# Moving the last transposes of a step and the preparation of the next tokens in an expert loop

## The chip, the cores and the metric

The kernel runs on one core of a Trainium2 chip. The metric is the device time of one execution in microseconds (us). Five engines run at once: TensorE (PE, matmuls and transposes), the vector engine (DVE), ScalarE (ACT), GpSimd (POOL) and SyncE (SP), which issues weight transfers. Each works through its own list in order and waits on semaphores that others raise.

## The reference

One layer of a diffusion backbone over 1024 latent tokens of width 1024, with a context of 256: modulation, RMSNorm, a combined projection, windowed and neighbourhood attention, an output projection, and then the part that matters here, a mixture of experts. Each token goes to 4 of 32 experts, and each expert computes

```
hu  = x @ w1[e] + b1[e]                       # 1024 -> 2048
glu = minimum(hu[:, 0::2], 7)
lin = clip(hu[:, 1::2], -7, 7)
act = glu * sigmoid(1.702 * glu) * (lin + 1)
y   = act @ w2[e] + b2[e]                     # 1024 -> 1024
```

The four results of a token are summed with softmax weights, normalised and added to the token. Everything is fp32.

## The kernel before

The kernel runs `front`, `attention`, `middle` (output projection, router, table of steps), `experts` and `combine`. The change is in `experts`.

**Steps.** Tokens of an expert stand in blocks of 128. A step handles one expert with R blocks: R = 1 (a one-block step) or R = 2 (a two-block step). A first loop runs 16 pairs, a one-block step and then a two-block step; a second loop runs 3 one-block steps. `body(st, next_r)` is the code of a step on one engine; `nxt` is the step behind it with `next_r` blocks.

**Units.** The weights of an expert are six units of 1024 x 512, four up (w1, n = 0 to 3) and two down (w2, n = 4, 5). Each is one transfer of 2 MB into a ring of three. fp32 is computed as high and low parts: ScalarE writes `w_hi` (L1256, `split`), the vector engine writes seven eighths of `w_lo` (L1311) and GpSimd the last eighth (L1208). A product of one unit and one block is 8 x 3 matmuls (L1402 to L1404), with a bias matmul ahead (L1418 up, L1436 down).

**Between up and down.** The result of up product j goes to the vector engine, which computes glu (L1356), lin (L1357, L1359) and, with ScalarE's sigmoid (L1286), act_o (L1361). `columns(st, j)` turns it for the down products: TensorE transposes act_o (L1389), ScalarE writes a_hi (L1265), the vector engine a_lo (L1321). It runs one product late: after product j come the columns of j - 1. The last j has no up product behind it. TensorE does it inside the first down unit, for the last block, ahead of k = 6; until then the down product needs only a_hi and a_lo of the earlier j.

**Between steps.** `rows(nxt, r)` prepares block r of the next step: TensorE transposes the gathered rows (L1382) into two PSUM banks, ScalarE writes x_hi (L1260), the vector engine x_lo (L1315). Row 0 follows the last up product, row 1 (if there is one) the first down product of block 0; TensorE's row r waits until x_lo of row r - 1 has been written. ScalarE and the vector engine do row 0 and the last `columns` ahead of their split at n = 4.

**The way back.** ScalarE copies each down product from its bank to y (L1295). There are two banks, so TensorE's down product i waits for the copy of product i - 2. GpSimd scatters y to memory and gathers the rows of the next step.

Of the kernel before, what the change touches and what calls it, by code (L numbers as in the profile page):

```python
# [28 lines left out]
KD = D // P  # L29
# [1053 lines left out]
def experts(K):  # L1083
# [3 lines left out]
    UP, DOWN = 2 * FF // UNIT, D // UNIT  # L1087
# [7 lines left out]
    with ctx:  # L1095
# [23 lines left out]
        at_done, ahi_done, a_ready = sem("at_done"), sem("ahi_done"), sem("a_ready")  # L1119
# [128 lines left out]
        @block.scalar  # L1248
        def _(act):
            act.sem_inc(y_copied, 2)  # L1250

            def split(st, n):
                wait_loaded(act, st, n)
                for c in range(CH):
                    k = slice(KC * c, KC * (c + 1))
                    act.activation(w_hi[:, n % HI, k, :], ring[:, n % RING, k, :], ACT.Copy).then_inc(hi_done, 1)  # L1256

            def rows(st, r):
                act.wait_ge(xt_done, st.blocks + r + 1)
                act.activation(x_hi[:, r, :, :].rearrange("p k n -> p (k n)"), ps[:, 6:8, :].rearrange("p b n -> p (b n)"), ACT.Copy).then_inc(xhi_done, 1)  # L1260

            def columns(st, j):
                act.wait_ge(at_done, UP * st.blocks + j + 1)
                n, r = divmod(j, st.R)
                act.activation(a_hi[:, r, 2 * n:2 * n + 2, :].rearrange("p k n -> p (k n)"), ps[:, 2 + j % 2, 0:2 * P], ACT.Copy).then_inc(ahi_done, 1)  # L1265

            first = Step(1, 0, 0)
            rows(first, 0)
            split(first, 0)
            split(first, 1)  # L1270

            def body(st, next_r):
                nxt = st.then(next_r)
                for n in range(NU):
                    if n == UP:
                        rows(nxt, 0)
                        columns(st, UP * st.R - 1)
                    act.wait_ge(prod_done, units_done(st, n))
                    if n + 2 < NU:
                        split(st, n + 2)  # L1280
                    else:
                        split(nxt, n + 2 - NU)
                    if n < UP:
                        for j in range(n * st.R, n * st.R + st.R):
                            act.wait_ge(glu_done, UP * st.blocks + j + 1)
                            act.activation(sig[:, j % 2, :], glu[:, j % 2, :], ACT.Sigmoid, scale=ALPHA).then_inc(sig_done, 1)  # L1286
                            if j:
                                columns(st, j - 1)
                        continue
                    if n == UP:  # L1290
                        act.wait_ge(y_free, st.passes + 1)
                    h = n - UP
                    for r in range(st.R):
                        wait_product(act, st, n, r)
                        act.activation(y[:, r, h * UNIT:(h + 1) * UNIT], ps[:, 4 + (h * st.R + r) % 2, :], ACT.Copy).then_inc(y_copied, 1)  # L1295
                        if n == UP and r + 1 < next_r:
                            rows(nxt, r + 1)

            program(act, body)

        @block.vector
        def _(dve):
            dve.sem_inc(lo_done, RING * CH)
            dve.sem_inc(up_free, 2)
            dve.sem_inc(a_ready, 2)

            def split(unit, n):
                for c in range(CH):
                    k = slice(KC * c, min(KC * (c + 1), KP))
                    dve.wait_ge(hi_done, CH * unit + c + 1)  # L1310
                    dve.tensor_tensor(w_lo[:, n % LO, k, :], ring[:, n % RING, k, :], w_hi[:, n % HI, k, :].bitcast(F32), ALU.subtract).then_inc(lo_done, 1)  # L1311

            def rows(st, r):
                dve.wait_ge(xhi_done, st.blocks + r + 1)
                dve.tensor_tensor(x_lo[:, r, :, :].rearrange("p k n -> p (k n)"), ps[:, 6:8, :].rearrange("p b n -> p (b n)"),  # L1315
                                  x_hi[:, r, :, :].bitcast(F32).rearrange("p k n -> p (k n)"), ALU.subtract).then_inc(x_ready, 1)

            def columns(st, j):
                dve.wait_ge(ahi_done, UP * st.blocks + j + 1)
                n, r = divmod(j, st.R)  # L1320
                dve.tensor_tensor(a_lo[:, r, 2 * n:2 * n + 2, :].rearrange("p k n -> p (k n)"), ps[:, 2 + j % 2, 0:2 * P],  # L1321
                                  a_hi[:, r, 2 * n:2 * n + 2, :].bitcast(F32).rearrange("p k n -> p (k n)"), ALU.subtract).then_inc(a_ready, 1)

            def select(sel, e, ready):

                col = onehot[:, bass.ds(e, 1)]
                dve.tensor_copy(sel[:, :], col.to_broadcast([96, P])).then_inc(ready, 1)

            first = Step(1, 0, 0)
            rows(first, 0)  # L1330
            dve.wait_ge(bias_loaded, 32)
            select(sel_up, expert_of(dve, first), sel_up_ready)
            split(0, 0)

            def body(st, next_r):
                nxt = st.then(next_r)
                unit = NU * st.passes
                link = linker(dve, dve_own, UP * st.blocks)
                e, e_next = expert_of(dve, st), expert_of(dve, nxt)
                for n in range(NU):  # L1340
                    if n == UP:
                        rows(nxt, 0)
                        columns(st, UP * st.R - 1)
                    dve.wait_ge(prod_done, units_done(st, n))
                    split(unit + n + 1, (n + 1) % NU)
                    if n == 0:
                        select(sel_down, e, sel_down_ready)
                    if n < UP:
                        for j in range(n * st.R, n * st.R + st.R):
                            s = j % 2  # L1350
                            pairs = ps[:, s, :].rearrange("p (j two) -> p j two", two=2)
                            wait_product(dve, st, n, j - n * st.R)
                            if j >= 2:

                                dve.wait_ge(at_done, UP * st.blocks + j - 1)
                            dve.tensor_scalar(glu[:, s, :], pairs[:, :, 0], LIMIT, None, ALU.min).then_inc(glu_done, 1)  # L1356
                            dve.tensor_scalar(lin[:, s, :], pairs[:, :, 1], LIMIT, -LIMIT, ALU.min, ALU.max).then_inc(up_free, 1)  # L1357
                            dve.wait_ge(up_free, UP * st.blocks + j + 3)
                            link(dve.scalar_tensor_tensor(lin[:, s, :], lin[:, s, :], 1.0, glu[:, s, :], ALU.add, ALU.mult))  # L1359
                            dve.wait_ge(sig_done, UP * st.blocks + j + 1)  # L1360
                            dve.tensor_tensor(act_o[:, s, :], lin[:, s, :], sig[:, s, :], ALU.mult).then_inc(act_done, 1)  # L1361
                            if j:
                                columns(st, j - 1)
                        if n == UP - 1:
                            select(sel_up, e_next, sel_up_ready)
                    elif n == UP:
                        for r in range(1, next_r):
                            rows(nxt, r)
                assert link.count[0] == UP * st.R

            program(dve, body)

        @block.tensor
        def _(pe):
# [17 lines left out]
            def product(st, n, r, bank, hi, lo, ready):  # L1392
                unit = NU * st.passes + n
                for c in range(CH):
                    if r == 0:
                        pe.wait_ge(lo_done, CH * unit + c + 1 + RING * CH)
                    for k in range(KC * c, KC * (c + 1)):
                        if r == 0 and k == KP:
                            pe.wait_ge(pool_lo_done, CH * unit + CH + RING * CH)
                        if ready:  # L1400
                            ready(k)
                        pe.matmul(bank, hi[:, r, k, :], w_hi[:, n % HI, k, :], start=False, stop=False)  # L1402
                        pe.matmul(bank, hi[:, r, k, :], w_lo[:, n % LO, k, :], start=False, stop=False)  # L1403
                        last = pe.matmul(bank, lo[:, r, k, :], w_hi[:, n % HI, k, :], start=False, stop=(k == KD - 1))  # L1404
# [4 lines left out]
            def body(st, next_r):  # L1409
                nxt = st.then(next_r)  # L1410
                ups = UP * st.R
                pe.wait_ge(sel_up_ready, st.passes + 1)
                for j in range(ups):
                    n, r = divmod(j, st.R)
# [5 lines left out]
                    if j:  # L1420
                        columns(st, j - 1)
                rows(nxt, 0)
                pe.wait_ge(sel_down_ready, st.passes + 1)

                for i in range(DOWN * st.R):
                    h, r = divmod(i, st.R)

                    def ready(k):
                        if k == KD - 2 and r == st.R - 1:
                            columns(st, ups - 1)  # L1430
                        if k % 2 == 0:
                            pe.wait_ge(a_ready, UP * st.blocks + (k // 2) * st.R + r + 3)

                    pe.wait_ge(y_copied, DOWN * st.blocks + i + 1)
                    bank = ps[:, 4 + i % 2, :]
# [113 lines left out]
```

## Time and profile before

| what | value |
|---|---|
| runs before | 3360.82, 3361.21, 3361.33 us (median 3361.21) |
| profiled execution, its own time | 3360.82 us |
| its span, first to last instruction | 3359.2 us |
| mean granted clock of TensorE | 0.944 of full speed |
| TensorE busy | 2876.1 us, 86% of the span |
| expert loop | about 1275 to 3274 us of the span |

### The profile page before, as it was taken

How to read it: one execution, taken by the hardware profiler on the slowest of the kernel's cores; microseconds unless marked ns; L12 is line 12 of the kernel's file. 1: busy time of each engine (PE TensorE's matmuls, PEld its weight loads, DVE VectorE, ACT ScalarE, POOL GpSimd, SP SyncE). 2: the span in 40 equal slices, each digit the busy share in tenths (PEclk: the TensorE clock that was granted, in tenths of full speed). 3: DMA queues.
4: the chain of work that ended last, by engine and by line, in shares of the span. 5: the costliest groups of instructions: out<-in, count | busy, mean ns of one | idle time of the engine just before them, and what ended most of it. 6: DMA issues, size and time to landing. Idle time of an engine off the chain costs nothing. (4 is left out here: it accounts for less than half of the span.)

```text
span 3359.2 us, 40318 instructions
## 1 busy us (share of the span) xinstructions
PE 2876.1 (86%) x13206; PEld 2162.3 (64%) x13207; DVE 1903.3 (57%) x2864; ACT 1400.2 (42%) x1667; POOL 831.9 (25%) x609
## 2 busy tenths in 40 slices
PE   4899979998957707999999999999999999999980
PEld 0254667777734405777777777777777777777760
DVE  0430024454422256677767776866776687667786
ACT  0100125555521105445544554554455455545551
POOL 1000021212211143224322322332232233323340
PEclk8999989999978858999999999999999999999995
DMA  9700032323132108568657766775676577667678
GB/s 248 252 26 25 13 94 56 77 49 87 45 105 75 75 8 308 211 219 300 229 209 262 266 229 225 267 267 207 225 287 230 219 275 256 222 228 281 241 284 312
DMA packets 285165, 629.36 MB, mean 187 GB/s; under 512 B 9922, under 2 KB 11202, under 8 KB 284962
## 3 DMA queue, kind: packets, MB, share of 16 engines
q1 hardware_dynamic: 261558, 549.12, 47.7%
q0 software_dynamic: 23568, 79.73, 6.6%
q8 instruction: 23, 0.38, 0.0%
q14 instruction: 16, 0.13, 0.0%
HBM read 584.63 MB, written 50.26 MB: 189 GB/s over the span
## 5 line engine op out<-in xcount | busy, mean ns | idle before, releaser
L1311 DVE TENSOR_TENSOR w_lo_x<-wring_x,w_hi_x 128x2048 fp32r<-128x2048 f32 (+1 forms) x422 | 885.1, 2145 | 118.5 <-PE psum L1404 113.1
L1256 ACT ACTIVATE w_hi_x<-wring_x 128x2048 fp32r<-128x2048 f32 x424 | 787.8, 1909 | 148.9 <-DMA wring_x<-in_w_mlp 148.7
L1402 PE MATMUL psum<-w_hi_x,x_hi_x 128*128 128x512 f32 x1632 | 676.4, 414 | 8.5 <-DVE w_lo_x L1311 8.5
L1404 PE MATMUL psum<-w_hi_x,x_lo_x 128*128 128x512 f32 x1632 | 637.2, 390 | 0.0
L1403 PE MATMUL psum<-w_lo_x,x_hi_x 128*128 128x512 f32 x1632 | 637.0, 390 | 0.0
L1208 POOL TENSOR_TENSOR w_lo_x<-wring_x,w_hi_x 128x512 fp32r<-128x512 f32 x212 | 312.9, 1480 | 864.0 <-ACT w_hi_x L1256 464.6
L1402 PE MATMUL psum<-w_hi_x,a_hi_x 128*128 128x512 f32 x816 | 346.2, 424 | 51.9 <-DVE a_lo_x L1321 50.3
L1402 PEld LDWEIGHTS psum<-w_hi_x,x_hi_x 128*128 128x128 f32 x1632 | 308.4, 189 | 69.6 <-DVE w_lo_x L1311 10.6
L1404 PEld LDWEIGHTS psum<-w_hi_x,x_lo_x 128*128 128x128 f32 x1632 | 306.9, 188 | 65.9
L1403 PEld LDWEIGHTS psum<-w_lo_x,x_hi_x 128*128 128x128 f32 x1632 | 307.7, 189 | 62.2
L1403 PE MATMUL psum<-w_lo_x,a_hi_x 128*128 128x512 f32 x816 | 322.1, 395 | 0.0
L1404 PE MATMUL psum<-w_hi_x,a_lo_x 128*128 128x512 f32 x816 | 321.8, 394 | 0.0
L1286 ACT ACTIVATE sig_x<-glu_x 128x256 f32<-128x256 f32 x204 | 84.5, 414 | 478.0 <-DVE glu_x L1356 477.7
L1402 PEld LDWEIGHTS psum<-w_hi_x,a_hi_x 128*128 128x128 f32 x816 | 156.1, 191 | 98.5 <-DVE a_lo_x L1321 65.0
L1356 DVE TENSOR_SCALAR glu_x<-psum 128x256 f32<-128x256 f32 x204 | 85.2, 418 | 231.4 <-PE psum L1404 231.3
L654 ACT ACTIVATE S<-S,negm 128x896 f32<-128x896 f32 (+1 forms) x128 | 119.6, 935 | 208.1 <-DVE negm L717 113.5
L465 PE MATMUL psum<-hT,ring 128*128 128x512 f32 (+1 forms) x496 | 201.2, 565 | 5.0 <-DVE hT L381 4.4
L630 PE MATMUL psum<-v,PT 128*128 (+1 forms) x1536 | 187.0, 273 | 0.0
L630 PEld LDWEIGHTS psum<-v,PT 128*128 128x128 f32 x1536 | 183.6, 194 | 0.0
L1404 PEld LDWEIGHTS psum<-w_hi_x,a_lo_x 128*128 128x128 f32 x816 | 155.1, 190 | 34.3
L1403 PEld LDWEIGHTS psum<-w_lo_x,a_hi_x 128*128 128x128 f32 x816 | 156.1, 191 | 29.6
L1321 DVE TENSOR_TENSOR a_lo_x<-psum,a_hi_x 128x256 fp32r<-128x256 f32 x204 | 85.1, 417 | 149.8 <-ACT a_hi_x L1265 149.8
(249 smaller groups left out, 3535.6 us busy)
## 6 DMA issues: line engine op xcount, KB each, us to landing
wring_x<-in_w_mlp SPq DMA_DIRECT2D x212, 2048.0 KB, 8.2
ring<-in_w_ada SPq DMA_DIRECT2D x12, 2048.0 KB, 9.5
bias<-bias_d SPq DMA_DIRECT2D x16, 1280.0 KB, 14.2
yg<-y_d SPq DMA_DIRECT2D x8, 2048.0 KB, 10.4
ring<-in_w_in SPq DMA_DIRECT2D x4, 2048.0 KB, 9.6
xin<-in_x SPq DMA_DIRECT2D x8, 512.0 KB, 5.1
ring<-in_w_out SPq DMA_DIRECT2D x2, 2048.0 KB
mix_d<-o SPq DMA_DIRECT2D x8, 512.0 KB, 6.6
```

Of the source, the lines that this page charges most:

```text
L465: last = pe.matmul(ps[:, g % 4, 0:width], lhs, rhs, start=(k == 0), stop=(k == KD - 1))
L630: last = pe.matmul(ps[:, 6 + s // NHA, head * HD:(head + 1) * HD], PT[:, s % 2, c * P:(c + 1) * P], v, start=(c == 0), stop=(c == chunks - 1))
L654: act.activation(S[:, s % 2, 0:keys(s)], S[:, s % 2, 0:keys(s)], ACT.Exp, bias=negm[:, s:s + 1], accum_out=den[:, s:s + 1]).then_inc(p_don ...
L1208: pool.tensor_tensor(w_lo[:, n % LO, KP:, :], ring[:, n % RING, KP:, :], w_hi[:, n % HI, KP:, :].bitcast(F32), ALU.subtract).then_inc(pool ...
L1256: act.activation(w_hi[:, n % HI, k, :], ring[:, n % RING, k, :], ACT.Copy).then_inc(hi_done, 1)
L1286: act.activation(sig[:, j % 2, :], glu[:, j % 2, :], ACT.Sigmoid, scale=ALPHA).then_inc(sig_done, 1)
L1311: dve.tensor_tensor(w_lo[:, n % LO, k, :], ring[:, n % RING, k, :], w_hi[:, n % HI, k, :].bitcast(F32), ALU.subtract).then_inc(lo_done, 1)
L1321: dve.tensor_tensor(a_lo[:, r, 2 * n:2 * n + 2, :].rearrange("p k n -> p (k n)"), ps[:, 2 + j % 2, 0:2 * P], a_hi[:, r, 2 * n:2 * n + 2, : ...
L1356: dve.tensor_scalar(glu[:, s, :], pairs[:, :, 0], LIMIT, None, ALU.min).then_inc(glu_done, 1)
L1402: pe.matmul(bank, hi[:, r, k, :], w_hi[:, n % HI, k, :], start=False, stop=False)
L1403: pe.matmul(bank, hi[:, r, k, :], w_lo[:, n % LO, k, :], start=False, stop=False)
L1404: last = pe.matmul(bank, lo[:, r, k, :], w_hi[:, n % HI, k, :], start=False, stop=(k == KD - 1))
```

## The change

Three things are moved; nothing is added to or taken from the computation.
- TensorE: `columns(st, ups - 1)`, the transposes of the last act_o, moves from inside the first down unit (last block, ahead of k = 6) to a place ahead of the first down product, behind `rows(nxt, 0)`.
- ScalarE: `rows(nxt, 0)` (x_hi) moves from ahead of the last `columns` to behind the split at n = 4.
- Vector engine: `rows(nxt, 0)` (x_lo) moves from ahead of the last `columns` to behind the split at n = 4, where the other rows are.

```diff
@@ scalar: body
                     if n == UP:
-                        rows(nxt, 0)
                         columns(st, UP * st.R - 1)
                     act.wait_ge(prod_done, units_done(st, n))
...
                     if n == UP:
+                        rows(nxt, 0)
                         act.wait_ge(y_free, st.passes + 1)
@@ vector: body
                     if n == UP:
-                        rows(nxt, 0)
                         columns(st, UP * st.R - 1)
...
                     elif n == UP:
-                        for r in range(1, next_r):
+                        for r in range(next_r):
                             rows(nxt, r)
@@ tensor: product
-                            ready(k)
+                            ready(k, r)
@@ tensor: body
                 rows(nxt, 0)
+                columns(st, ups - 1)
                 pe.wait_ge(sel_down_ready, st.passes + 1)
+                def ready(k, r):
+                    if k % 2 == 0:
+                        pe.wait_ge(a_ready, UP * st.blocks + (k // 2) * st.R + r + 3)
 
                 for i in range(DOWN * st.R):
                     h, r = divmod(i, st.R)
-                    def ready(k):
-                        if k == KD - 2 and r == st.R - 1:
-                            columns(st, ups - 1)
-                        if k % 2 == 0:
-                            pe.wait_ge(a_ready, UP * st.blocks + (k // 2) * st.R + r + 3)
```

## Rows read from the trace of the kernel before

**Rows 1.** The page, busy times of the engines.
```profile
PE 2876.1 (86%) x13206; PEld 2162.3 (64%) x13207; DVE 1903.3 (57%) x2864; ACT 1400.2 (42%) x1667; POOL 831.9 (25%) x609
```

**Rows 2.** Waits, 1300 to 3260 us: total us, times, longest.
```profile
ACT w_hi_x L1256 <- DMA wring_x<-in_w_mlp: 139.3, 67, 3.5
...
PE psum L1402 <- DVE a_lo_x L1321: 50.3, 49, 1.7
...
PE psum L1436 <- ACT y_x L1295: 31.6, 16, 2.0
...
PE psum L1382 <- DMA xg_x<-h_d,record_x: 22.9, 17, 2.3
```

**Rows 3.** Timeline, TensorE, end of a two-block step: start, duration.
```profile
1956.57 0.38 PE L1436 MATMUL psum<-btab_x,sel_down_x 96*128 96x512 bf16 x1
...
1966.60 0.38 PE L1389 MATMUL psum<-ident,act_o_x 128*128 128x128 f32 x2
1967.91 0.50 PE L1402 MATMUL psum<-w_hi_x,a_hi_x 128*128 128x512 f32 x1 [0.93 <-DVE a_lo_x L1321]
1971.54 0.39 PE L1436 MATMUL psum<-btab_x,sel_down_x 96*128 96x512 bf16 x1 [1.97 <-ACT y_x L1295]
1977.23 0.39 PE L1436 MATMUL psum<-btab_x,sel_down_x 96*128 96x512 bf16 x1
1982.93 0.39 PE L1418 MATMUL psum<-btab_x,sel_up_x 96*128 96x512 bf16 x1
```

**Rows 4.** Timeline of the other engines, same step.
```profile
1955.88 1.28 POOL L1208 TENSOR_TENSOR w_lo_x<-wring_x,w_hi_x 128x512 fp32r<-128x512 f32 x1 [10.51 <-PE psum L1404]
1956.47 0.97 DVE L1359 SCALAR_TENSOR_TENSOR lin_x<-lin_x,glu_x 128x256 f32<-128x256 f32 x1
1957.48 0.42 DVE L1361 TENSOR_TENSOR act_o_x<-lin_x,sig_x 128x256 f32<-128x256 f32 x1
...
1970.89 1.07 ACT L1295 ACTIVATE y_x<-psum 128x512 f32<-128x512 f32 x2
```

**Rows 5.** Timeline, TensorE, end of a one-block step.
```profile
2009.06 0.38 PE L1436 MATMUL psum<-btab_x,sel_down_x 96*128 96x512 bf16 x1
...
2015.21 0.38 PE L1389 MATMUL psum<-ident,act_o_x 128*128 128x128 f32 x2
...
2018.02 1.03 PE L1382 MATMUL psum<-ident,xg_x 128*128 128x128 f32 x8
2018.89 0.38 PE L1436 MATMUL psum<-btab_x,sel_down_x 96*128 96x512 bf16 x1
2024.58 0.39 PE L1418 MATMUL psum<-btab_x,sel_up_x 96*128 96x512 bf16 x1
```

**Rows 6.** Timeline of the other engines, same step.
```profile
2012.90 0.43 DVE L1361 TENSOR_TENSOR act_o_x<-lin_x,sig_x 128x256 f32<-128x256 f32 x1
...
2015.63 0.38 ACT L1265 ACTIVATE a_hi_x<-psum 128x256 fp32r<-128x256 f32 x1 [1.92 <-PE psum L1389]
...
2019.52 0.59 ACT L1295 ACTIVATE y_x<-psum 128x512 f32<-128x512 f32 x1
2019.99 1.02 ACT L1260 ACTIVATE x_hi_x<-psum 128x1024 fp32r<-128x1024 f32 x1
...
2021.05 1.23 DVE L1315 TENSOR_TENSOR x_lo_x<-psum,x_hi_x 128x1024 fp32r<-128x1024 f32 x1 [0.71 <-ACT x_hi_x L1260]
```

**Rows 7.** Timeline, one-block step of the second pattern.
```profile
2240.84 0.38 PE L1436 MATMUL psum<-btab_x,sel_down_x 96*128 96x512 bf16 x1
...
2243.24 0.43 DVE L1361 TENSOR_TENSOR act_o_x<-lin_x,sig_x 128x256 f32<-128x256 f32 x1
...
2254.91 0.39 PE L1418 MATMUL psum<-btab_x,sel_up_x 96*128 96x512 bf16 x1
```

**Rows 8.** Stretches: us, PE, PEld, DVE, ACT, POOL busy; granted clock, DMA share, GB/s.
```profile
1621.20:1625.20 4.00, 3.69 (x11) 2.93 (x12) 4.00 (x3) 4.00 (x4) 1.64 (x1) 0.63 0.44 144
```

**Rows 9.** Timeline, TensorE, third and fourth down product of such a step.
```profile
1621.51 0.39 PE L1436 MATMUL psum<-btab_x,sel_down_x 96*128 96x512 bf16 x1 [1.98 <-ACT y_x L1295]
...
1628.84 0.39 PE L1436 MATMUL psum<-btab_x,sel_down_x 96*128 96x512 bf16 x1
```

## The prediction

> **What bounds the kernel now.** I read the page's busy times first: TensorE is busy 86% of the span, the vector engine 57%, ScalarE 42% [rows 1]. The reader should see that in the expert loop only time in which TensorE stands still, or runs slowly, can be won. Then the view of waits over the loop (1300 to 3260 us) [rows 2]. TensorE waits there 50.3 us for the low half of the activations (a_lo), 31.6 us for ScalarE's copy of y, and 22.9 us for gathered rows. These are the waits that the edit can touch. Then the timeline around the end of a step, once for a two-block step [rows 3, 4] and once for a one-block step [rows 5, 6]. The 16 two-block steps look alike. The one-block steps come in two patterns; [rows 7] is of the second, found in 5 of the 16 that are paired with a two-block step. Three more one-block steps follow at the end of the loop.
>
> **Two-block step (16 of them).** Before: the last transposes of activations (`columns` of the last j, L1389) sit inside the second down product, ahead of k = 6. They start at 1966.60 and the next matmul only at 1967.91, since ScalarE must write a_hi and the vector engine a_lo first. ScalarE stood at the same `columns` in its own order, so it splits the next weights late and copies y only at 1970.89 [rows 4]; TensorE's third down product waits for that until 1971.54 [rows 3]. One product takes 5.69 us (1977.23 to 1982.93, with its bias matmul). From 1956.57 to the next step's first matmul at 1982.93 are 26.36 us for four products of 22.77 us, so 3.6 us are transposes and stalls.
>
> After: TensorE must have act_o before the first down product. act_o ends at 1957.90 (1957.48 + 0.42) [rows 4], and TensorE follows 0.06 us later, so it stands from 1956.57 to 1957.96, 1.4 us. Then 0.22 us of transposes, four products, 0.1 us of restart: the next step begins at 1981.0 instead of 1982.93. a_hi, a_lo and the y copy are then done during the first down product: ScalarE needs about 0.4 + 3.7 + 1.0 us for a_hi, split and x_hi, less than 5.69. Gain 1.9 us, x16 = 30.4 us. The cover of the two moved `rows(nxt, 0)` is ample here: the next step is two to three products away.
>
> The vector engine's part of that wait is stretched. L1359 takes 0.97 us, beside a GpSimd split from 1955.88 to 1957.16 [rows 4], against 0.42 us elsewhere. The Trainium skill (GPSIMD Engine Reference, section 1, Specifications) says that GpSimd and the vector engine contend for SBUF when the vector instruction has two SBUF inputs, which L1359 has; by that rule the stretch stays, and the wait is 1.4 us. With 0.42 us it would be 0.85 us and the total 9 us lower. I take the row as it is, since nothing in the edit moves either instruction.
>
> **One-block step followed by a two-block step (16).** Here the vector engine is late, not TensorE: the down product begins at 2009.06 [rows 5] while the last act_o is finished only at 2013.33 (2012.90 + 0.43) [rows 6]. Before, TensorE worked through k = 0 to 5 in that time, with short stalls. After, it stands from 2009.06 to 2013.39, 4.3 us; 2.9 us in the second pattern (2240.84 to 2243.73) [rows 7]. Call the end of this wait S.
> - The first down product then has all it needs: 0.22 + 5.69 = S + 5.91.
> - `rows(nxt, 1)` on TensorE waits for x_lo of row 0, which is now queued behind ScalarE's split of the next weights. From transposes to a_hi 0.42 us (2015.21 to 2015.63), from a_hi through the split to the next ScalarE instruction 3.89 (2015.63 to 2019.52), x_hi to x_lo 1.06 (2019.99 to 2021.05), x_lo 1.23, hand-over 0.05 [rows 5, 6]: S + 6.65. So 0.74 us more waiting.
> - Transposes 0.87 (2018.02 to 2018.89) and the second product 5.69: the next step begins at S + 13.21.
> That is 2026.60 against 2024.58: +2.0 us. In the second pattern 2243.73 + 13.21 = 2256.94 against 2254.91 [rows 7]: +2.0 us as well. Four of the 16, where the gathered rows came late, lose some 0.5 us less. Sum +30. In the second pattern ScalarE's split may also meet its transfer not yet landed; an estimate of 0.3 us for 5 steps, +1.5.
>
> What is queued behind the two waits: on TensorE nothing but its own products; on ScalarE the copy of y, which has its bank free until the step after; on the vector engine, x_lo now stands behind a 3.95 us split, which ends at about S + 5.1, before x_hi is there. On the DMA queue the load that needs this split goes out earlier (in the two-block step some 8 us earlier than at 1971.9), with no one short of it.
>
> **The last three one-block steps.** No `rows(nxt, 1)`: S + 0.22 + 11.38, about +0.7 us each, +2.
>
> **The clock.** The rows show a second cost. In 5 of the 16 two-block steps the product after the y wait ran 7.33 us instead of 5.69 (1621.51 to 1628.84) [rows 9], +1.6 us, and the granted clock of that stretch is 0.63 of full speed [rows 8]: part of it at the lower level, 1.2 GHz, after TensorE had stood 0.93 and 1.98 us within five. The edit takes these two waits away: -8 us, with the caveat that the new wait of 1.4 us could bring one or two back. But the one-block step now has a gap of 2.9 to 4.3 us, longer than any in the loop before and right behind the wait for gathered rows. If 2.9 us in pieces is followed by the lower clock 5 times in 16, I expect it behind nearly every one of these gaps. One such stretch costs 1.6 us; 0.74 of it hides in the wait for x_lo; so 0.9 us, or up to 2.5 if two stretches follow each other. I take 1.0 for the 16, and 1.6 for the last three: +21. Bounds: nothing, and 16 x 2.5 + 3 x 3.3 = 50.
> The Trainium skill (TensorE: Matmul & The Clock Gate, section "HAM oscillation") speaks against this change: waits between bursts of matmuls throttle the engine, and the next burst starts at 1.2 GHz. By it the sum is the one below; without it the sum is 21 us lower.
>
> **Sum**, against the profiled execution's 3360.8 us (0.4 under the median of the runs): -30.4 -8 +30 +1.5 +2 +21 = +16: 3377 us.
>
> **Rivals.**
> A. The lower clock does not come behind the new gaps. Then -5: 3356 us, no change that can be told (within 0.2%, 6.7 us, about what a measurement of this kernel tells). For it: waits of 2.1 to 2.3 us for gathered rows mostly left the clock alone before. Against it: the new gaps are up to twice as long. 20%.
> B. On the other side, faster: the split of the weights in the one-block step now waits for its transfers (ScalarE waits for weights 139.3 us in all [rows 2]). If the earlier loads take this away, the last act_o comes earlier. With 2.5 us each for the 16 steps: -40, 3337 us. It decides from 1.4 us a step on. Against it: the load for the fifth unit waits for a GpSimd split that stands behind the scatter of y, whose place is the same. 8%.
> C. Two stretches at the lower clock behind most gaps, 3395 us or so. 12%.
> D. The forecast, 60%.
>
> **How the numbers follow.** Predicted is D, 3377, its own range 3369 to 3386. The range reaches to A and part of C: 3354 to 3390. Slower by over 0.2%: C and most of D, 0.68. Within: A and a little of D, 0.23. Faster: B and an edge of A, 0.09.
>
> **What the changed profile would show.** The wait of L1436 for y gone; waits of L1402 for a_lo gone; a wait of L1389 for act_o of about 1.4 us in each two-block step and 3 to 4.3 us in each one-block step, some 90 us in all; two-block steps of 72.3 us (before 74.3 or 75.9); one-block steps of 43 to 45 us (before 40.2 or 41.7); a wait of L1382 for x_lo near 0.7 us where the clock stayed up; a granted clock under 1 behind the one-block gaps. Wrong would make it: act_o earlier than in [rows 6], a clock that stays up, or a wait that I costed at nothing, such as x_lo for the next step's first product.

## The result, and the profile after

The changed kernel takes 3383.48 us (median of five runs, 3374.20 to 3387.11) against 3361.21 (3360.82 to 3361.33): ratio 1.006, 95% interval 1.0041 to 1.008. It is slower, by 22 us. The forecast was 3377, in a range of 3354 to 3390. The profiled execution took 3385.55 us, its span 3383.9.

The page of the changed kernel, busy times:

```profile
PE 2891.7 (85%) x13206; PEld 2182.2 (64%) x13207; DVE 1887.1 (56%) x2864; ACT 1407.9 (42%) x1667; POOL 866.9 (26%) x609
```

The waits of TensorE's matmuls and of ScalarE's split in the changed kernel, 1300 to 3285 us (total, times, longest):

```profile
PE psum L1389 <- DVE act_o_x L1361: 97.2, 48, 5.5
...
ACT w_hi_x L1256 <- DMA wring_x<-in_w_mlp: 93.4, 48, 3.8
...
PE psum L1382 <- DMA xg_x<-h_d,record_x: 18.8, 16, 1.7
...
PE psum L1382 <- DVE x_lo_x L1316: 6.6, 6, 1.9
```

Two rows of [rows 2] are gone: the 50.3 us of L1402 for a_lo and the 31.6 us of L1436 for y, 81.9 us together. In their place stand 97.2 us of L1389 for act_o, and 6.6 us for x_lo. By these waits alone that is 22 us more. That this is also the difference of the two times is chance: the clock has a share of its own, and smaller terms go the other way, as the steps show.

The timeline of TensorE, end of a two-block step of the changed kernel, against [rows 3]:

```profile
1733.06 1.04 PE L1382 MATMUL psum<-ident,xg_x 128*128 128x128 f32 x8
1735.31 0.44 PE L1389 MATMUL psum<-ident,act_o_x 128*128 128x128 f32 x2 [1.21 <-DVE act_o_x L1361]
1735.59 0.38 PE L1436 MATMUL psum<-btab_x,sel_down_x 96*128 96x512 bf16 x1
1741.27 0.39 PE L1436 MATMUL psum<-btab_x,sel_down_x 96*128 96x512 bf16 x1
1746.96 0.39 PE L1436 MATMUL psum<-btab_x,sel_down_x 96*128 96x512 bf16 x1
1752.66 0.39 PE L1436 MATMUL psum<-btab_x,sel_down_x 96*128 96x512 bf16 x1
1758.35 0.39 PE L1418 MATMUL psum<-btab_x,sel_up_x 96*128 96x512 bf16 x1
```

One wait of 1.21 us, and then four products of 5.69 us without a stop; the granted clock stays at 1 in all 16 two-block steps. ScalarE copies y at 1741.47, 5.5 us before the bank is wanted; in [rows 4] the copy came late.

The same of a one-block step, against [rows 5]:

```profile
1783.55 1.09 PE L1382 MATMUL psum<-ident,xg_x 128*128 128x128 f32 x8 [1.16 <-DMA xg_x<-h_d,record_x]
1788.80 0.69 PE L1389 MATMUL psum<-ident,act_o_x 128*128 128x128 f32 x2 [4.16 <-DVE act_o_x L1361]
1789.28 0.63 PE L1436 MATMUL psum<-btab_x,sel_down_x 96*128 96x512 bf16 x1
...
1790.14 0.63 PE L1403 MATMUL psum<-w_lo_x,a_hi_x 128*128 128x512 f32 x1
...
1796.64 1.03 PE L1382 MATMUL psum<-ident,xg_x 128*128 128x128 f32 x8
1797.51 0.38 PE L1436 MATMUL psum<-btab_x,sel_down_x 96*128 96x512 bf16 x1
1803.19 0.39 PE L1418 MATMUL psum<-btab_x,sel_up_x 96*128 96x512 bf16 x1
```

TensorE stands 4.16 us, and the matmuls behind the gap take 0.63 us instead of 0.39. Why act_o comes so late stands in the timelines of the other engines in this step:

```profile
1774.34 3.73 ACT L1256 ACTIVATE w_hi_x<-wring_x 128x2048 fp32r<-128x2048 f32 x2 [2.54 <-DMA wring_x<-in_w_mlp]
...
1777.97 0.40 ACT L1285 ACTIVATE sig_x<-glu_x 128x256 f32<-128x256 f32 x1
...
1778.47 3.43 DVE L1361 TENSOR_TENSOR act_o_x<-lin_x,sig_x 128x256 f32<-128x256 f32 x1 [0.46 <-ACT sig_x L1285]
...
1779.06 2.55 POOL L1208 TENSOR_TENSOR w_lo_x<-wring_x,w_hi_x 128x512 fp32r<-128x512 f32 x2
...
1782.15 5.01 DVE L1312 TENSOR_TENSOR w_lo_x<-wring_x,w_hi_x 128x2048 fp32r<-128x2048 f32 x2
1787.09 0.41 DVE L1356 TENSOR_SCALAR glu_x<-psum 128x256 f32<-128x256 f32 x1
...
1788.32 0.42 DVE L1361 TENSOR_TENSOR act_o_x<-lin_x,sig_x 128x256 f32<-128x256 f32 x1
```

The last up product had ended by 1781.95. Its glu waited behind a 5.01 us split of the first down unit. That split began late because the act_o of the product before stood ahead of it: it waited for a sigmoid that stood behind ScalarE's split of a unit just landed, and then took 3.43 us beside two of GpSimd's splits. All of this was so before the change too (in the step of [rows 6], act_o 3.43 us at 2003.02 and a split of 5.04 us at 2006.71); TensorE then had other work. And the stretches around the gap (us, PE, PEld, DVE, ACT, POOL busy; granted clock, DMA share, GB/s):

```profile
1770.00:1780.00 10.00, 10.00 (x48) 8.24 (x46) 9.44 (x12) 4.99 (x6) 6.82 (x6) 1.00 1.03 382
1789.30:1792.70 3.40, 3.40 (x9) 2.63 (x8) 2.76 (x3) 3.17 (x3) 0.00 (x0) 0.50 1.04 388
...
1794.00:1803.00 9.00, 9.00 (x46) 7.49 (x44) 5.69 (x5) 5.65 (x5) 1.29 (x1) 1.00 0.71 252
```

The table has the time from the first matmul of each step (L1418) to that of the next, summed over the 16 pairs of the profiled execution, then that execution's own time and the median of the runs. The medians of the experiments are from other runs, beside which the kernel before took 3362.1 to 3363.2 us (medians); the ratios below are against those. A profiled execution can lie some us off its kernel's median, most of all with the gap filled (5 under) and with block 0, k = 4 (8 over).

| kernel | 16 one-block steps, us | 16 two-block steps, us | profiled execution, us | median, us |
|---|---|---|---|---|
| before | 671.6 | 1196.2 | 3360.8 | 3361.2 |
| changed | 731.7 | 1157.2 | 3385.6 | 3383.5 |
| TensorE's part only | 723.8 | 1157.2 | 3381.1 | 3379.2 |
| order of the other engines only | 770.5 | 1227.8 | 3493.7 | 3489.9 |
| two-block steps only | 670.9 | 1157.4 | 3326.2 | 3326.9 |
| one-block steps only | 731.9 | 1193.0 | 3421.6 | 3423.1 |
| changed, gap filled | 712.6 | 1157.4 | 3364.9 | 3370.3 |
| block 0, k = 6 | 673.4 | 1134.8 | 3302.0 | 3302.9 |
| block 0, k = 4 | 654.5 | 1144.2 | 3293.7 | 3285.6 |
| changed, activation ahead of split | 721.4 | 1157.3 | 3378.7 | 3379.7 |
| block 0, k = 4, activation ahead of split | 724.0 | 1134.8 | 3366.8 | 3368.0 |
| block 0, k = 4 or 6 | 650.9 | 1142.8 | 3283.3 | 3283.8 |

So the change is a gain of 39 us in the two-block steps and a loss of 60 us in the paired one-block steps. The last three one-block steps (+4.3 us), the first pair's later start (+1.3) and the end behind the last down product (-1.9) make up the rest of the 24.7 us between the spans.

### The profile page after: what moved, and what is told of

The parts are those of the page before. It is cut to its first block and busy times, and to the rows that moved or that the text cites. A ratio compares the mean times of both kernels' runs of the same rounds, so it can differ in the third digit from the quotient of the medians.

```text
span 3383.9 us, 40318 instructions
## 1 busy us (share of the span) xinstructions
PE 2891.7 (85%) x13206; PEld 2182.2 (64%) x13207; DVE 1887.1 (56%) x2864; ACT 1407.9 (42%) x1667; POOL 866.9 (26%) x609
## 5 line engine op out<-in xcount | busy, mean ns | idle before, releaser
L1312 DVE TENSOR_TENSOR w_lo_x<-wring_x,w_hi_x 128x2048 fp32r<-128x2048 f32 (+1 forms) x422 | 874.0, 2115 | 195.8 <-PE psum L1404 191.5
L1402 PE MATMUL psum<-w_hi_x,x_hi_x 128*128 128x512 f32 x1632 | 676.6, 415 | 5.6 <-DVE w_lo_x L1312 5.6
L1208 POOL TENSOR_TENSOR w_lo_x<-wring_x,w_hi_x 128x512 fp32r<-128x512 f32 x212 | 327.8, 1550 | 888.3 <-PE psum L1404 810.5
L1402 PE MATMUL psum<-w_hi_x,a_hi_x 128*128 128x512 f32 x816 | 353.5, 433 | 0.0
L1402 PEld LDWEIGHTS psum<-w_hi_x,x_hi_x 128*128 128x128 f32 x1632 | 308.4, 189 | 65.9 <-DVE w_lo_x L1312 6.5
L1403 PE MATMUL psum<-w_lo_x,a_hi_x 128*128 128x512 f32 x816 | 329.9, 404 | 0.0
L1356 DVE TENSOR_SCALAR glu_x<-psum 128x256 f32<-128x256 f32 x204 | 85.7, 420 | 270.5 <-PE psum L1404 270.2
L1402 PEld LDWEIGHTS psum<-w_hi_x,a_hi_x 128*128 128x128 f32 x816 | 162.4, 199 | 32.9
L1204 POOL TENSOR_TENSOR poolgate_x<-poolgate_x 128x1 f32<-128x1 f32 x70 | 96.0, 1372 | 341.7 <-ACT y_x L1296 246.0
```

The costliest lines, as they stand in the source:

```text
L1204: pool.tensor_tensor(poolgate[:, 1:2], poolgate[:, 0:1], poolgate[:, 0:1], ALU.add).then_inc(gate_open, 1)
L1208: pool.tensor_tensor(w_lo[:, n % LO, KP:, :], ring[:, n % RING, KP:, :], w_hi[:, n % HI, KP:, :].bitcast(F32), ALU.subtract).then_inc(pool ...
```

## The experiments

Theory T: the loss is TensorE's wait for the last act_o in one-block steps, with the lower clock behind it; the gain is ScalarE and the vector engine set free earlier in two-block steps. Rival R: the loss is x_hi and x_lo, which now queue behind the splits.

**TensorE's part only.** The diff of TensorE as in the change, the other two engines as before.

> Only TensorE's part of the change: the last transposes ahead of the first down product in all steps, ScalarE and the vector engine in the order of before. Theory T (the loss is TensorE's wait for act_o in one-block steps, with the lower clock behind it): nearly as slow as the full change; the waits for x_lo (6.6 us) go, one-block steps near 44.5 us, two-block steps 72.3 us; total 3372 to 3384. Rival R (the loss is x_hi and x_lo queued behind the splits): the loss is gone and the two-block gain of 39 us stays; total about 3325.

3379.2 us (3377.6 to 3381.1; ratio 1.0046, 1.003 to 1.0063). As T has it, and R is out as the main cause: with x_hi and x_lo back in their old place, 52 of the 60 us lost in one-block steps stay. The waits of the matmuls in this kernel, same view:

```profile
PE psum L1389 <- DVE act_o_x L1361: 94.3, 45, 5.3
PE psum L1382 <- DMA xg_x<-h_d,record_x: 22.1, 17, 2.8
```

The wait for x_lo is gone, and one-block steps are 0.5 us shorter on the mean (7.9 us over 16).

**Order only.**

ScalarE's and the vector engine's diffs as in the change, TensorE as before:

```diff
@@ scalar: body
                     if n == UP:
-                        rows(nxt, 0)
                         columns(st, UP * st.R - 1)
...
                     if n == UP:
+                        rows(nxt, 0)
                         act.wait_ge(y_free, st.passes + 1)
@@ vector: body
                     if n == UP:
-                        rows(nxt, 0)
                         columns(st, UP * st.R - 1)
...
                     elif n == UP:
-                        for r in range(1, next_r):
+                        for r in range(next_r):
                             rows(nxt, r)
```

> Only the order on ScalarE and the vector engine is changed (x_hi and x_lo behind the splits), TensorE's last transposes stay inside the first down unit. T: ScalarE is still held at the last transposes, and x_lo comes 0.4 + 3.9 + 1.1 + 1.2 us after them, so the second row's transposes wait some 3.8 us in each paired one-block step: about +55 to +60 us, 3415 to 3422; two-block steps change by under 1 us each. R: the same +60. A third view, that the order is free because x_lo is not needed until the next step: 3361.

3489.9 us (3487.1 to 3493.7; ratio 1.0374, 1.0357 to 1.0392). The direction was right and the size expected was half of what came: +127 us, not +60. TensorE's timeline in a one-block step of this kernel (transposes of act_o are L1388 here, of gathered rows L1381):

```profile
1939.47 0.38 PE L1388 MATMUL psum<-ident,act_o_x 128*128 128x128 f32 x2
...
1946.10 1.97 PE L1381 MATMUL psum<-ident,xg_x 128*128 128x128 f32 x8 [3.66 <-DVE x_lo_x L1315]
1947.86 0.63 PE L1435 MATMUL psum<-btab_x,sel_down_x 96*128 96x512 bf16 x1
```

The wait of 3.66 us is the one worked out (3.8). Two things were left out: behind it the matmuls again run at 0.63 us, and in the two-block step ScalarE now does x_hi ahead of the y copy, so that wait grows from 1.97 to 2.9 us and the lower clock follows it in all 16. The table has it: +98.9 us over 16 one-block steps (6.2 each) and +31.6 over 16 two-block steps (2.0 each), where +55 to +60 and under 1 us each were expected. The order of the other engines is thus safe only together with the earlier transposes.

**Two-block steps only, and one-block steps only.** The full change under `if st.R == 2`, and under `if st.R == 1`.

> The full change in two-block steps only, one-block steps as before. T: two-block steps 72.3 us instead of 74.3 or 75.9, one-block steps stay at 40 to 42: -39 us, 3322. R says the same for the two-block steps. If parts of the loss come from the two-block steps (earlier transfers that collide later), more than 3330.

> The full change in one-block steps only. T: one-block steps near 45 us, two-block steps 74.3 or 75.9 as before: +60 to +64 us, 3421 to 3426. If the two halves don't add up to the full change (+22), the parts interact.

3326.9 us (5 above the figure expected; 3320.2 to 3328.6; ratio 0.9888, 0.9869 to 0.9907) and 3423.1 us (3421.6 to 3429.0; ratio 1.0184, 1.0166 to 1.0203). The ratios add to +0.72%, the full change has +0.6% with an interval of 0.41 to 0.80%: the halves do not interact in a way that can be told. In the table each half leaves the other kind of step within 3.3 us of before over 16 steps; those 3.3 us are fewer stretches at the lower clock behind the y wait (three instead of five).

**The gap filled.** In one-block steps of the changed kernel:

```diff
                 rows(nxt, 0)
+                if st.R == 1:
+                    pe.wait_ge(sel_down_ready, st.passes + 1)
+                    pe.wait_ge(y_copied, DOWN * st.blocks + 1)
+                    for _ in range(10):
+                        pe.matmul(ps[:, 4, :], sel_down[:, :], btab[:, 2 * FF:2 * FF + UNIT], start=True, stop=True)
                 columns(st, ups - 1)
```

> The full change, and in one-block steps ten extra bias matmuls (2.1 us at the full clock) into a free bank, while TensorE would wait for the last act_o; their result is overwritten. They add no time of their own where the gap is at least 2.2 us. Theory T (the lower clock behind the gap costs about 1.6 us per one-block step): the granted clock stays at full speed, the time falls by 15 to 25 us against the full change, to about 3358 to 3368. Rival (the clock costs nothing on the chain, only the wait does): no change, 3375 to 3387.

3370.3 us (3362.5 to 3376.6, eight runs; ratio 1.0025, 1.0012 to 1.0038): 13 us under the changed kernel, 2 us above the range expected, and the intervals of the two ratios do not meet. The timeline of TensorE in a one-block step of this kernel (the fillers are L1426, the down products L1439):

```profile
1891.75 2.32 PE L1426 MATMUL psum<-btab_x,sel_down_x 96*128 96x512 bf16 x10
1896.31 0.44 PE L1388 MATMUL psum<-ident,act_o_x 128*128 128x128 f32 x2 [2.23 <-DVE act_o_x L1360]
1896.58 0.38 PE L1439 MATMUL psum<-btab_x,sel_down_x 96*128 96x512 bf16 x1
1903.00 1.09 PE L1381 MATMUL psum<-ident,xg_x 128*128 128x128 f32 x8 [0.58 <-DVE x_lo_x L1315]
1903.93 0.38 PE L1439 MATMUL psum<-btab_x,sel_down_x 96*128 96x512 bf16 x1
```

and its stretch behind the gap (columns as above):

```profile
1896.50:1901.50 5.00, 5.00 (x24) 4.16 (x24) 4.51 (x5) 4.72 (x4) 0.00 (x0) 1.00 1.01 380
```

TensorE does useless work, act_o comes no sooner (over the 16 steps its place sums to within 0.1 us of the changed kernel's), and the step is faster: in 15 of the 16 steps no matmul of the first down product ran at the lower clock, where in the changed kernel some did in all 16. From the first to the second down product are 7.35 us here; in the changed kernel 8.23 (1789.28 to 1797.51) and 8.7 on the mean of 15 steps. And the wait for x_lo comes out (0.58 us) where the clock stays up: the two costs hide each other in part, as worked out. In 6 of those 15 steps the profile still has a stretch at the lower clock ahead of the gap's end.

**Block 0 instead of the last block.** The kernel before, with one condition changed:

```diff
-                        if k == KD - 2 and r == st.R - 1:
+                        if k == KD - 2 and r == 0:
```

> The kernel before with one word changed: the last transposes sit at k = 6 of block 0 instead of the last block. One-block steps unchanged. T: in two-block steps act_o has long been written there, and ScalarE gets free a product earlier: the wait for a_lo goes (block 0 needs the last a_lo of its own j only), the wait for the y copy goes; step about 71.0 us. 16 x 3.4 and the 5 x 1.6 of the clock: -55 to -62 us, 3299 to 3306. Rival: ScalarE copies y late for another reason, then the wait of L1436 stays and only 17 us are won, 3344.

3302.9 us (3302.0 to 3307.4; ratio 0.9827, 0.981 to 0.9843). Two-block steps take 70.9 us each, with no wait at all in their down part; the gathered rows and a_lo in one-block steps remain. In two-block steps this is where both goals meet: late enough for act_o to be there, early enough to set ScalarE free.

**Block 0, ahead of k = 4.**

```diff
-                        if k == KD - 2 and r == st.R - 1:
+                        if k == KD - 4 and r == 0:
```

> As the first-block version, but ahead of k = 4 instead of k = 6. T: in one-block steps TensorE waits there for a_lo of the j before anyway, act_o is ready by then, and the 0.93 us wait at k = 6 is hidden by the six matmuls of k = 4 and 5: another -1.0 us in 19 one-block steps, 3280 to 3288. Rival: act_o is not ready at k = 4 and the wait only moves: same as the first-block version.

3285.6 us (3279.5 to 3293.7; ratio 0.9765, 0.9748 to 0.9781). The waits of the matmuls in this kernel:

```profile
PE psum L1382 <- DMA xg_x<-h_d,record_x: 22.2, 16, 2.2
PE psum L1402 <- DVE w_lo_x L1311: 13.8, 17, 1.9
PE psum L1389 <- issue: 13.6, 12, 1.4
```

The wait for a_lo is gone. The 13.6 us put down to issue end 0.1 us behind act_o's end each time, so TensorE still waits for act_o there, 1.0 to 1.4 us in 9 of the 16 one-block steps. Against k = 6, one-block steps win 19 us over 16; two-block steps give 9 us back, in waits for w_lo at their start: they now begin before the vector engine has split their first unit.

**Activation ahead of the split.** In one-block steps the vector engine does glu, lin and act_o of the last up product first, then splits the first down unit; once on the changed kernel and once on the version with k = 4.

```diff
+                    late = n == UP - 1 and st.R == 1
+                    if not late:
-                    split(unit + n + 1, (n + 1) % NU)
+                        split(unit + n + 1, (n + 1) % NU)
...
+                        if late:
+                            split(unit + n + 1, (n + 1) % NU)
                         if n == UP - 1:
                             select(sel_up, e_next, sel_up_ready)
```

> The full change, and in one-block steps the vector engine computes the last glu, lin and act_o before it splits the first down unit instead of after. Theory T (the length of TensorE's new wait is the 4 to 6 us that the vector engine spends on that split first): act_o is ready about 25.5 us into the step instead of 30.4, the wait of L1389 for act_o falls from 97 us to under 35 us, and a wait of L1402 for w_lo of 1.5 to 3 us appears in each one-block step, since the split is now last; the total falls by 10 to 35 us against the full change, to 3350 to 3373. Rival (the vector engine is late because of GpSimd or a transfer, whatever its order): wait and time as with the full change, 3375 to 3387.

> The version with the last transposes ahead of k = 4 of block 0, with the same order of the vector engine in one-block steps. T: the waits for act_o and a_lo vanish, the wait for w_lo of the first down unit is in their place; between -20 and +10 us against 3286, so 3266 to 3296. If act_o was the only thing late: -20; if the split is as late as act_o was: 0.

3379.7 us (3373.9 to 3382.6; ratio 1.005) and 3368.0 us (3364.0 to 3371.1; ratio 1.002). The first moved the wait as foreseen, but by less, and its time is 7 us above T's range and inside the rival's: next to nothing is won. The rival is still not the explanation, since act_o came 1.6 to 3.4 us earlier in 15 of the 16 one-block steps than in the same steps of the kernel before. Its waits:

```profile
PE psum L1392 <- DVE act_o_x L1362: 47.1, 43, 5.6
PE psum L1405 <- DVE w_lo_x L1311: 30.1, 19, 1.9
```

Half of the wait for act_o turned into one for w_lo, and the clock still drops. The vector engine's timeline shows why act_o was not there at once:

```profile
1896.02 0.43 DVE L1360 SCALAR_TENSOR_TENSOR lin_x<-lin_x,glu_x 128x256 f32<-128x256 f32 x1
1897.61 1.28 DVE L1362 TENSOR_TENSOR act_o_x<-lin_x,sig_x 128x256 f32<-128x256 f32 x1 [1.16 <-ACT sig_x L1285]
```

It waits for a sigmoid that stands on ScalarE behind a split. The second version missed its range by 72 us: with act_o needed only at k = 4 nothing is won by having it earlier, while the wait for w_lo is 71.4 us, 22 times, with the lower clock behind. In a one-block step the vector engine as a whole is late, whichever of the two it does first; the split is what the down product needs first.

**Both places.** k = 4 in one-block and k = 6 in two-block steps.

> Last transposes in block 0, ahead of k = 4 in one-block steps and of k = 6 in two-block steps. T: the same as k = 4 throughout, 3280 to 3290, since in two-block steps both places are later than act_o; the 0.2 to 1.9 us waits for w_lo at the start of two-block steps come from the one-block step's earlier end and stay. Rival (k = 4 in the two-block step disturbs something): 5 us or more faster.

3283.8 us (3282.6 to 3286.9; ratio 0.977, 0.9753 to 0.9786), the same as k = 4 throughout (3279.5 to 3293.7). The place in the two-block step makes no difference, and the waits for w_lo at its start stay.

## Why the prediction was right, point by point

- **Two-block step.** Forecast 72.3 us, measured 72.33 in the mean; the wait for act_o 1.4 us forecast, 1.21 in the profile. Gain 38 us forecast, 39 measured over the 16 steps; 36 us as a kernel of its own (3326.9 against 3363.2). The vector engine's instruction beside GpSimd's split stayed stretched (0.96 us), as the row had it.
- **One-block step, the wait.** The last act_o is ready 30.4 us from the step's start (1788.74 less 1758.35), as in [rows 5, 6] (2013.33 in a step that begins at 1982.93 [rows 3]); TensorE's stop of 4.3 us is there (4.16 us ahead of L1389 at 1788.80). That this stop is the loss is shown by the version with TensorE's part only. The forecast put a step's end at S + 13.21 us at the full clock. With S from each of the 16 steps of the kernel before, that makes a loss of 30.3 us, against 30 forecast. From one kernel to the other act_o moved by 1.8 us in sum, against the 1.5 us put down for a transfer not yet landed. That is luck in part: it came up to 1.5 us later in some steps and up to 1.1 us earlier in others. And the second pattern is in 4 of the 16 steps before the change, not in 5.
- **x_lo behind the split.** Forecast 0.74 us where the clock stays up: 0.58 with the gap filled, and 6.6 us in all in the changed kernel, 7.9 us when it is undone. Right.
- **The clock.** Forecast as the second cost and confirmed by filling the gap. Its size was the term that was too small. I took 1.0 us for a paired step, after hiding. From the first to the second down product the changed kernel takes 8.7 us on the mean, where the step shown with the gap filled takes 7.35: 1.35. Transposes and restart at the lower clock add 0.2 (0.48 us from 1788.80 to 1789.28, against 0.28 us in the two-block step). So about 1.6 instead of 1.0. The whole remainder says the same: one-block steps cost +60.1 us where the sum had +47.5 (+30 +1.5 +16); less 30.3 and 1.8, 27.9 us are left, 1.7 a step. With the gap filled, 9.0 us are left by the same sum, so some 19 of the 27.9 us are shown to be the clock; the rest was not told apart. The other half of the clock term came out as forecast: the 5 slow stretches of the two-block steps are gone, and the new wait of 1.2 us brought none back. One reading was loose: the gap was called longer than any in the loop before, but the first step of the loop before has one of 6.45 us, for w_lo.
- **The last three steps.** +7 forecast, +4.3 measured up to the last down product.
- **The rivals.** A (clock stays up, 3356) did not happen; the version with the gap filled is 13 us better than the measurement, and it does not keep the clock up everywhere. B (faster through earlier transfers): the wait of ScalarE for weights did fall, from 139.3 to 93.4 us, but act_o came no earlier in most one-block steps. The fifth unit's load went out behind GpSimd's split, 8.0 us into the step in both kernels (1766.33 less 1758.35; 1990.90 less 1982.93), which is what was held against B. C (two stretches behind most gaps, 2.5 us a step) was nearer to the truth than its 12% say: the 1.7 us left per step lie midway between one stretch (0.9) and two, and only one step of the 16 lost more than 2.5.
- **The sum.** The profiled execution is 24.7 us longer where the sum had 16. The paired one-block steps were put 12.6 us too low, the last three 2.5 us too high, the two-block steps 0.7 us too high; the start and the end, put at nothing, come to -0.6 us.
- What stays open: the changed kernel's five runs spread over 13 us, those of before beside them over 0.5. Beside the experiments the kernel before itself spread over 10 us and more (3359.6 to 3369.9), so no cause is claimed.

## What to carry to other kernels

A wait that is put into an in-order queue must be costed at the point where the awaited thing is ready in each kind of step; here the same edit won 2.4 us in one kind and lost 3.8 in the other. Look for the place that is late enough for the producer and early enough for whoever is held behind it: one condition in the old kernel (block 0, k = 4) gave 2.3% where the change lost 0.6%. An idle gap on TensorE can cost more than its length: here the matmuls behind every gap of 2.3 to 5.5 us for act_o ran at the lower clock, and those behind the gaps of 1.2 us did not. Count both.

## What was not expected of the hardware

- Ten useless matmuls in the gap (2.32 us) made the kernel 13 us faster, with the clock at 1.00 behind the gap instead of 0.50 in 15 of 16 steps.
- Gaps of 2.3 to 5.5 us for act_o, in 15 of the 16 paired steps with a wait for gathered rows of 0.7 to 1.8 us shortly before, were followed by 0.63 us matmuls in every one-block step of the changed kernel. In three of them the clock had already fallen ahead of the gap. Before the change, waits of up to 2.3 us for gathered rows were followed by the lower clock in 2 of 16 steps.
- Vector instructions with two SBUF inputs were held up beside GpSimd's split far beyond their own length: act_o took 3.43 us (1778.47) where it takes 0.42. Over the loop of the kernel before, lin (L1359) took 0.42 to 0.43 us in all 105 cases clear of a GpSimd split, and 0.66 to 3.04 us in 95 of the 96 that overlap one; glu (L1356), which reads PSUM, took 0.41 to 0.43 us in either case.
